# A two-block transformer kernel on one core: the first mixer's head norm and gating spread over three engines, level sums by halves, two modulation rows moved, and both output projections in three rounded passes

## The chip, the core and the metric

The kernel runs on one core of a Trainium2 chip. Its engines work in parallel, each through its own list of instructions in order, and wait for one another on semaphores: TensorE (PE in the profile, with PEld for its weight loads), VectorE (DVE), ScalarE (ACT), GpSimd (POOL) and SyncE (SP), which here only issues transfers. The metric is the device time of one launch, in microseconds.

## What is computed

Two transformer blocks in float32 for 256 tokens of width 1024. The first one has a feed-forward layer, a mixer and a second feed-forward layer, all modulated by nine rows made from a conditioning vector `c`; the second has another mixer and a layer that picks experts. The parts that matter here, cut:

```python
# modulation: nine rows of 1024, 18 tiles of 512 columns in the kernel
mod = (silu(c) @ ada_w + ada_b); (sh1, sc1, g1, sh2, sc2, g2, sh3, sc3, g3) = split(mod, 9)

def head_rmsnorm(h, g, n_heads):            # over 128 columns of each head
    hf = h.reshape(B, S, n_heads, W // n_heads)
    hf = hf * rsqrt(mean(hf * hf, axis=-1, keepdims=True) + EPS)
    return hf.reshape(B, S, W) * g

def token_mix(...):                         # the first mixer
    hm = mlstm_chunkwise(q, k, v, log_i, log_f)          # 4 heads, "scores"
    out_m = head_rmsnorm(hm, mnorm_g, 4) * sigmoid(mo)
    ho = hgrn2_chunkwise(hq_, hk_, hv_, hlf)             # 4 heads, "scan"
    out_h = head_rmsnorm(ho, hnorm_g, 4) * silu(hg)
    return concatenate([out_m, out_h]) @ w_out           # output projection 1

# second block
merged = sigmoid(gate_fox) * (y_fox @ p_fox) + sigmoid(gate_rwkv) * (y_rwkv @ p_rwkv)
x = layer_norm(alpha * x + merged @ w_o, ...)            # output projection 2
```

## The kernel before, in words

**Tiles.** The 256 tokens are two tiles (`TT` = 2) of 128 partitions, the width is eight tiles of 128 (`KT` = 8). All weights of the stages up to the experts form one stream of 1 MB chunks. SyncE loads them in order into a ring of four slots. Chunk g may be loaded when chunk g-3 has begun on TensorE (semaphore `begun`). So what follows a chunk in the stream is fetched only as TensorE goes on.

**Two ways to multiply.** In the plain way float32 operands go to TensorE, and each matmul stands in the trace as two records. In the other, `three_passes` (lines 375 to 377), each operand is a rounded top and a rounded rest, and three matmuls give top by top, top by rest and rest by top. The top of a chunk is made by two ScalarE copies (`top_chunk_act`, line 342), the rest by two VectorE subtractions (`rest_chunk_dve`, line 353), and for the first chunk of some stages by two GpSimd subtractions (`first_rest_pool`, line 951). The feed-forward and input projections are in three passes. The two output projections (`output_pe`, line 590) are plain: eight of the width tiles, two token tiles and two halves of 512 columns make 32 matmuls each.

**The first mixer**, after its input projections:
- *Scores.* `M_SEQ` gives the order in which TensorE works: S (scores of a head, lines 1170 and 1171), T (its transposition, 1176), N (values, 1183 to 1185). VectorE weights the scores, ScalarE copies the transposed ones, and VectorE writes each head's result into `yb` (1424).
- *Scan.* Eight steps i, four heads by two token tiles. TensorE makes the decays of step i+1 (`decays`, 1192), ScalarE takes their exponentials (1306), VectorE multiplies them into queries and keys (`decay`, 1433 and 1435), TensorE multiplies these at eight levels (`attend`, 1208), VectorE masks (`mask`, 1444) and adds the eight levels with one reduction (1451), TensorE multiplies by the values (`read_out`, 1219 and 1221) and VectorE copies out (1458). Steps 1 and 3 also host modulation tiles 14 and 15 (`LOOPED`).
- *Tail.* After the last step TensorE computes modulation tiles 12 and 13 (`BEHIND["scan"]`; one is a group of matmuls with weights from two chunks, lines 667 and 674, and a sum, line 681). Meanwhile VectorE squares all heads (1473), adds (1474), asks ScalarE for the root, and for each token tile multiplies by the inverse root, the gain and the gate (1477 to 1480). TensorE transposes the result, ScalarE copies it to `yT`, and the output projection runs.

**The second mixer** ends similarly. After a long recurrence in four groups VectorE normalises the last group (`group_scale_dve` 1682, 1683, `group_finish_dve` 1689 to 1693), TensorE multiplies it (line 1925, four parts), VectorE merges (2165, 2168), TensorE transposes, and the second output projection starts. GpSimd has nothing to do in either mixer, apart from the first rest of a stage.

## Time and profile before

| what | us |
|---|---|
| median of three runs | 1899.54 (1897.96 to 1906.75) |
| the profiled execution | 1899.65 |
| its span, first to last instruction | 1897.9 |
| TensorE busy | 1785.5 (94%) |
| scores of the first mixer | 368.5 to 380.3 |
| its scan | 380.3 to 430.4 |
| its tail, to the start of the output projection | 430.4 to 445.1 |
| first output projection | 445.1 to 472.8 |
| second output projection | 997.0 to 1024.7 |

The profiled execution is 1.75 us longer than its span. The stages' bounds are read from the instructions in order of time.

### The profile page before, as it was taken

Reading aid. Unit: us, or ns where it says so; the run is one execution under the profiler, and the core shown is the slowest. Engines: PE = TensorE matmul, PEld = TensorE weight load, DVE = VectorE, ACT = ScalarE, POOL = GpSimd, SP = SyncE. Lnnn points to the kernel's source line nnn. Section 1 sums busy time; section 2 is a strip of 40 time slices with the busy share of each in tenths; the row PEclk is TensorE's granted clock in tenths of the full one; section 3 lists DMA queues with packets and bytes.
Section 4 is the critical chain, followed back from the end, with each engine's and each line's share of the span. In section 5 each row is a group of like instructions: output and inputs, shape, how many; then the busy total and the mean of one; then the engine's idle time right before and its main releaser. Section 6 shows DMA issues by size and latency. Waiting matters only on the chain.

```text
span 1897.9 us, 32765 instructions
## 1 busy us (share of the span) xinstructions
PE 1785.5 (94%) x12730; PEld 1552.3 (82%) x12730; DVE 1181.6 (62%) x2035; ACT 764.8 (40%) x1164; POOL 339.9 (18%) x314
## 2 busy tenths in 40 slices
PE   6899989898899989998988999999999999999997
PEld 3899769763799879877855999899999988888885
DVE  3777547594555445874553399948888954444444
ACT  3343344522544445641102454454444443333334
POOL 1000000000000000000000077830000045555553
PEclk9999989999999989999998999999999999999999
DMA  7776555325655534440013445554444466666664
GB/s 305 286 284 246 207 196 178 133 89 210 222 177 177 190 112 139 161 144 21 3 45 133 157 145 169 165 155 146 141 142 141 145 183 194 190 196 190 195 191 155
DMA packets 62368, 315.97 MB, mean 166 GB/s; under 512 B 6928, under 2 KB 7344, under 8 KB 41008
## 3 DMA queue, kind: packets, MB, share of 16 engines
q1 hardware_dynamic: 60912, 305.94, 48.8%
q10 hardware_dynamic: 1280, 8.39, 1.2%
q8 instruction: 84, 1.38, 0.3%
q14 instruction: 28, 0.23, 0.0%
q0 software_dynamic: 64, 0.04, 0.0%
HBM read 313.29 MB, written 1.05 MB: 166 GB/s over the span
## 4 chain that ended last, share of the span: by engine, by line
PE 76%; DVE 9%; DMA 7%; ACT 4%; POOL 2%; issue 2%; SPq 0%; DVEq 0%; POOLq 0%; ACTq 0%
PE bank L375 20%; PE bank L376 20%; PE bank L377 20%; DMA ring<-in_stream 5%; PE bank L590 3%; PE bank L2327 3%; DVE ring_rounded L353 2%; DVE field L845 2%; POOL ring_rounded L2619 1%; DMA ring<-in_experts 1%; ACT arena_rounded L342 1%; PE bank L2301 1%; PE bank L536 1%; PE bank L1925 1%; PE bank L1738 1%
## 5 line engine op out<-in xcount | busy, mean ns | idle before, releaser
L377 PE MATMUL bank<-yb_rounded,ring_rounded 128*128 128x256 f32 x2080 | 595.7, 286 | 0.0
L377 PEld LDWEIGHTS bank<-yb_rounded,ring_rounded 128*128 128x128 f32 x2080 | 406.6, 195 | 0.0
L2425 ACT CAST ring_rounded<-ring 128x1024 fp32r<-128x1024 f32 x250 | 262.5, 1051 | 279.3 <-DMA ring<-in_experts 279.3
L353 DVE TENSOR_TENSOR ring_rounded<-ring,arena_rounded 128x1024 fp32r<-128x1024 f32 x218 | 256.9, 1221 | 163.6 <-ACT arena_rounded L342 163.4
L375 PE MATMUL bank<-yb_rounded,arena_rounded 128*128 128x256 f32 x1104 | 323.3, 293 | 21.5 <-POOL ring_rounded L951 8.2
L376 PE MATMUL bank<-yT_rounded,arena_rounded 128*128 128x256 f32 x1104 | 320.1, 290 | 0.0
L375 PE MATMUL bank<-yb_rounded,ring_rounded 128*128 128x256 f32 x976 | 283.2, 290 | 9.1 <-POOL ring_rounded L2619 6.5
L342 ACT CAST arena_rounded<-ring 128x1024 fp32r<-128x1024 f32 x222 | 221.3, 1047 | 142.0 <-PE bank L375 112.3
L2578 DVE TENSOR_TENSOR ring_rounded<-ring,ring_rounded 128x1024 fp32r<-128x1024 f32 x128 | 157.1, 1227 | 191.7 <-ACT ring_rounded L2425 191.7
L376 PE MATMUL bank<-yT_rounded,ring_rounded 128*128 128x256 f32 x976 | 275.9, 283 | 0.0
L376 PE MATMUL bank<-ring_rounded,arena_rounded 128*128 128x512 f32 x688 | 267.8, 389 | 0.0
L375 PEld LDWEIGHTS bank<-yb_rounded,arena_rounded 128*128 128x128 f32 x1104 | 220.2, 199 | 26.5 <-issue 9.9
L2619 POOL TENSOR_TENSOR ring_rounded<-ring,ring_rounded 128x1024 fp32r<-128x1024 f32 x46 | 125.3, 2738 | 640.6 <-ACT ring_rounded L2425 640.6
L376 PEld LDWEIGHTS bank<-yT_rounded,arena_rounded 128*128 128x128 f32 x1104 | 219.9, 199 | 0.5
L375 PE MATMUL bank<-ring_rounded,arena_rounded 128*128 128x512 f32 x512 | 199.6, 390 | 1.1 <-POOL arena_rounded L2637 1.1
L377 PE MATMUL bank<-ring_rounded,arena_rounded 128*128 128x512 f32 x512 | 199.3, 389 | 0.0
L375 PEld LDWEIGHTS bank<-yb_rounded,ring_rounded 128*128 128x128 f32 x976 | 186.7, 191 | 11.7 <-ACT field L2436 6.5
L376 PEld LDWEIGHTS bank<-yT_rounded,ring_rounded 128*128 128x128 f32 x976 | 187.0, 192 | 0.2
L2634 POOL CAST arena_rounded<-field 128x256 fp32r (+1 forms) x128 | 100.4, 784 | 409.0 <-PE bank L375 409.0
L376 PEld LDWEIGHTS bank<-ring_rounded,arena_rounded 128*128 128x128 f32 x688 | 129.2, 188 | 26.9 <-issue 0.5
L375 PEld LDWEIGHTS bank<-ring_rounded,arena_rounded 128*128 128x128 f32 x512 | 96.1, 188 | 22.6 <-issue 2.8
L377 PEld LDWEIGHTS bank<-ring_rounded,arena_rounded 128*128 128x128 f32 x512 | 96.1, 188 | 20.1
(411 smaller groups left out, 2611.5 us busy)
## 6 DMA issues: line engine op xcount, KB each, us to landing
ring<-in_stream SPq DMA_DIRECT2D x160, 1024.0 KB, 4.9
ring<-in_experts SPq DMA_DIRECT2D x256, 512.0 KB, 3.6
field<-in_gains ACTq DMA_DIRECT2D x1, 2048.0 KB, 7.9
field<-in_gains ACTq DMA_DIRECT2D x1, 1536.0 KB, 6.5
const<-in_const SPq DMA_DIRECT2D x1, 1474.0 KB, 7.9
xh<-in_x ACTq DMA_DIRECT2D x1, 1024.0 KB, 5.6
field<-in_gains ACTq DMA_DIRECT2D x2, 512.0 KB, 6.8
field<-in_norms ACTq DMA_DIRECT2D x1, 1024.0 KB, 9.0
```

The source lines that it names most:

```text
L342: nc.scalar.copy(top, ring[:, g % SLOTS, half * HALF:(half + 1) * HALF]).then_inc(sem("weight_top_ready"), 1)
L353: ins = nc.vector.tensor_tensor(ring_r[:, g % SLOTS, half], ring[:, g % SLOTS, half], top.bitcast(F32), ALU.subtract)
L375: first = pe.matmul(bank, s_top, m_top, start=start, stop=False)
L376: pe.matmul(bank, s_top, m_rest, start=False, stop=False)
L377: return first, pe.matmul(bank, s_rest, m_top, start=False, stop=stop)
L590: ins = pe.matmul(four[2 * t + n][:, :], yT[:, c + k, t * P:(t + 1) * P], w[:, k, :], start=(c + k == 0), stop=(c + k == KT - 1))
L845: nc.vector.scalar_tensor_tensor(row(tile), w[:, k, :], col("c")[:, 4 * c + k:4 * c + k + 1], row(tile), ALU.mult, ALU.add).then_inc(sem(" ...
L2327: ins = pe.matmul(bank[:, q * P:(q + 1) * P], hot[:, g % 2, 0, q, :], hot[:, g % 2, 1, q, :], start=True, stop=True)
L2425: nc.scalar.copy(expert_top[:, n % E_SLOTS, :], expert_w[:, n % E_SLOTS, :]).then_inc(expert_top_ready, 1)
L2578: vec.tensor_tensor(expert_rest[:, slot, :], expert_w[:, slot, :], expert_top[:, slot, :].bitcast(F32), ALU.subtract).then_inc(v_split, 1)
L2619: nc.gpsimd.tensor_tensor(expert_rest[:, slot, :], expert_w[:, slot, :], expert_top[:, slot, :].bitcast(F32), ALU.subtract).then_inc(u_spl ...
L2634: nc.gpsimd.tensor_copy(h_top[:, b, :], src).then_inc(h_top_ready, 1)
```

## The change

Five things are edited.

1. **Head squares on ScalarE, gates on GpSimd.** The squares of each head are summed by ScalarE as the head is done (`score_squares_act`, `loop_squares_act`). GpSimd first multiplies the gates by the gains (two instructions of 1024 elements per partition) and then each finished head by its gate (four instructions of 256, eight of 128). Of the tail are left the root, one reciprocal and one multiplication per token tile.
2. **Level sums by halves.** Two additions (512, then 256 elements) take the place of the reduction of 1024. They leave two partial sums, and `read_out` does one more matmul in each step.
3. **Modulation tiles 12 and 13** move from behind the scan into `M_SEQ`, between the scores. Their chunks move forward in the stream.
4. **Output projections in three rounded passes**, with splits of their four chunks and of the transposed activations.
5. **Early splits.** The first chunk of output projection 1 gets its top at step 5 of the scan and its rest from GpSimd. The first two of projection 2 get theirs behind the last root of the recurrence's norm, also with GpSimd.

The core of the diff:

```diff
     for k in range(4):
-        ins = pe.matmul(four[2 * t + n][:, :], yT[:, c + k, t * P:(t + 1) * P], w[:, k, :],
-                        start=(c + k == 0), stop=(c + k == KT - 1))
+        ins, last = three_passes(pe, four[2 * t + n][:, :], (y_top[:, t, c + k, :], y_rest[:, t, c + k, :]), w[k],
+                                 c + k == 0, c + k == KT - 1)
...
+        def gate_heads_pool(pool):
+            pool.wait_ge(sem("norms_in"), 16)
+            for n, gates in enumerate(("score_gates", "loop_gates")):
+                pool.wait_ge(*marks[gates])
+                at = slice(n * W1, (n + 1) * W1)
+                nc.gpsimd.tensor_tensor(mixg[:, :, at], mixg[:, :, at], norms[:, at].unsqueeze(1).broadcast_to([P, TT, W1]),
+                                        ALU.mult).then_inc(sem("gates_scaled"), 1)
...
+            for i in range(HEADS * TT):
+                if i == 5:
+                    first_rest_pool(pool, "out", "mixed")
+                pool.wait_ge(sem("h_squared"), i + 1)
...
+                nc.gpsimd.tensor_tensor(yb[:, t, at], yb[:, t, at], mixg[:, t, at], ALU.mult).then_inc(sem("h_gated"), 1)
...
         def read_out(i):
-                ins = pe.matmul(bank[:, 0:P], att[:, 0, i % 2, :], val[:, t, :], start=True, stop=not t)
+                pe.matmul(bank[:, 0:P], att[:, i % 2, 0, :], val[:, t, :], start=True, stop=False)
+                ins = pe.matmul(bank[:, 0:P], att[:, i % 2, 1, :], val[:, t, :], start=False, stop=not t)
...
         def mix_act(act):       # in the scan's loop over i
+                if i < 2:
+                    score_squares_act(2 + i)
+                if i >= 3:
+                    loop_squares_act(i - 3)
+                if i == 5:
+                    first_top_act(act, "out", "mixed")
...
         def mask(i):
-                vec.tensor_reduce(att[:, 0, i % 2, :], masked.rearrange("p l s -> p s l"), AX_X, ALU.add
+                v(vec.tensor_tensor(masked[:, 0:4, :], masked[:, 0:4, :], masked[:, 4:8, :], ALU.add))
+                vec.tensor_tensor(att[:, i % 2, 0:2, :], masked[:, 0:2, :], masked[:, 2:4, :], ALU.add
                                   ).then_inc(sem("h_att"), 1)
...
             for t in range(TT):
-                v(vec.tensor_tensor(by_head[:, t], by_head[:, t],
-                                    small[:, 160 + t * 8:168 + t * 8].unsqueeze(2).broadcast_to([P, 8, P]), ALU.mult))
-                v(vec.tensor_tensor(yb[:, t, :], yb[:, t, :], norms[:, 0:D], ALU.mult))
-                vec.tensor_tensor(yb[:, t, :], yb[:, t, :], mixg[:, t, :], ALU.mult).then_inc(sem("y_mixed"), 1)
+                vec.tensor_tensor(by_head[:, t], by_head[:, t], head_inverse[:, t, :].unsqueeze(2).broadcast_to([P, 2 * HEADS, P]),
+                                  ALU.mult).then_inc(sem("y_mixed"), 1)
+            after_first_rest_dve("out", "mixed")
+            turn_split_dve(dve, turned_at["mixed"])
+            for _ in range(3):
+                rest_chunk_dve(dve)
...
         def mix2_act(act):
             group_root_act(act, NCH // GRP - 1)
-            turn_act(act)
+            first_top_act(act, "out2", "merged", 2)
+            top_chunk_act(act, 3)
+            turn_split_act(act)
+            for gap in (0, 1):
+                top_chunk_act(act, gap)
```

**Order, TensorE among the scores.** Before, from the first transposed head (L1176 is T, L1170 and L1171 are S, L1183 to L1185 are N):

```order
L1176 MATMUL bank<-const,field 128x128 x3
L1170 MATMUL bank<-field 128x128
L1171 MATMUL bank<-field 128x256
L1183 MATMUL bank<-field 128x128
L1184 MATMUL bank<-field 128x128
L1185 MATMUL bank<-field 128x128
L1176 MATMUL bank<-const,field 128x128 x3
```

Now, from the same place (L1204 is T, L1198 and L1199 are S, L1211 to L1213 are N, L667 and L674 a modulation tile, L681 its sum):

```order
L1204 MATMUL bank<-const,field 128x128 x3
L667 MATMUL bank<-ring,tiny 32x512 x8
L674 MATMUL bank<-field,tiny 32x512
L1198 MATMUL bank<-field 128x128
L1199 MATMUL bank<-field 128x256
L1211 MATMUL bank<-field 128x128
L1212 MATMUL bank<-field 128x128
L1213 MATMUL bank<-field 128x128
L1204 MATMUL bank<-const,field 128x128 x3
L681 MATMUL bank<-field,const 128x512
```

A modulation tile now stands between the first transposition and the third head's scores, and its sum behind the second transposition. Tile 13 follows in the same way before the third N, and its sum before the last.

**Order, GpSimd, from the start to the experts.** Before:

```order
L2725 MEMSET field 128x7168
L2727 DMA field<-in_ada_b 1x16x448
L951 ISA
L951 TENSOR_TENSOR ring_rounded<-ring,arena_rounded 128x1024 x4
L2619 TENSOR_TENSOR ring_rounded<-ring,ring_rounded 128x1024 x46
```

Now:

```order
L952 ISA
L952 TENSOR_TENSOR ring_rounded<-ring,arena_rounded 128x1024 x2
L1109 TENSOR_TENSOR field<-field 128x2x512 x2
L1115 TENSOR_TENSOR yb<-yb,field 128x2x128 x4
L1122 TENSOR_TENSOR yb<-yb,field 128x128 x5
L952 TENSOR_TENSOR ring_rounded<-ring,arena_rounded 128x1024 x2
L1122 TENSOR_TENSOR yb<-yb,field 128x128 x3
L952 TENSOR_TENSOR ring_rounded<-ring,arena_rounded 128x1024 x6
L2702 TENSOR_TENSOR ring_rounded<-ring,ring_rounded 128x1024 x46
```

Between the input stage's rest (the first two of L952) and the experts there are now fourteen gate instructions and, besides the two for the second feed-forward layer, six subtractions of 1024 elements for the output projections.

**Order, ScalarE at the end of the second mixer.** Before, from the last copy of the recurrence:

```order
L1805 COPY field<-bank 128x4x4x16
L1660 ACTIVATE field<-field 128x4x64
L525 COPY yT<-bank 128x4x128 x4
L2022 DMA field<-in_lns 128x2048
L456 ACTIVATE field,small<-xh 128x512
```

Now:

```order
L1879 COPY field<-bank 128x4x4x16
L1734 ACTIVATE field<-field 128x4x64
L348 CAST arena_rounded<-ring 128x1024 x4
L512 CAST yb_rounded<-bank 128x512 x4
L348 CAST arena_rounded<-ring 128x1024 x4
L2101 DMA field<-in_lns 128x2048
```

Four of the casts stand directly behind the last root (L1660 before, L1734 now); the GpSimd subtractions wait for them.

## Rows read from the trace of the kernel before

**Rows 1.** Stage table, scan: from:to, length, PE, PEld, DVE, ACT, POOL busy, PE clock, DMA.

```profile
382.00:430.00 48.00, 41.30 (x244) 29.18 (x242) 46.14 (x55) 12.19 (x24) 0.00 (x0) 0.96 0.24 88
```

**Rows 2.** Instructions in order of time, PE, end of the scores: start, length, idle before.

```profile
379.51 0.49 PE L1183 MATMUL bank<-field 128*128 128x128 f32 x2 [0.57 <-ACT field L1301]
...
380.28 3.17 PE L1192 MATMUL bank<-const,field 128*128 128x512 f32 x8
```

**Rows 3.** Chain of waits: a modulation tile in the scan, and its sum.

```profile
390.90 1.85 PE bank L667 x16
392.75 0.84 PE bank L674 x2
...
397.97 0.86 PE bank L681 x2
```

**Rows 4.** Groups of the scan: busy, mean ns, idle before and its releaser.

```profile
L1451 DVE TENSOR_REDUCE field<-field 128x128 f32<-128x1024 f32 x8 | 15.4, 1923 | 0.3
...
L1208 PE MATMUL bank<-field 128*128 128x128 f32 x128 | 17.2, 292 | 3.3 <-DVE field L1438 2.1 <-DVE field L1435 0.9 <-DVE field L1444 0.3
```

**Rows 5.** In order of time: ends of the tail on DVE, then the projection.

```profile
430.44 2.29 DVE L1473 TENSOR_TENSOR field<-yb 128x2048 f32<-128x2048 f32 x1
...
442.01 1.22 DVE L1480 TENSOR_TENSOR yb<-yb,field 128x1024 f32<-128x1024 f32 x1
...
445.11 27.73 PE L590 MATMUL bank<-ring,yT 128*128 128x512 f32 x64 [0.72 <-ACT yT L525]
```

**Rows 6.** One pass of 512 columns (chain), and a chunk's two casts on ACT.

```profile
367.32 0.23 PE bank L375
...
1012.77 1.99 ACT L342 CAST arena_rounded<-ring 128x1024 fp32r<-128x1024 f32 x2
```

**Rows 7.** DVE and POOL where both work, in time; one line's min/median/max.

```profile
1136.71 2.38 POOL L2619 TENSOR_TENSOR ring_rounded<-ring,ring_rounded 128x1024 fp32r<-128x1024 f32 x1 [0.32 <-ACT ring_rounded L2425]
...
1136.77 4.46 DVE L2503 TENSOR_TENSOR field<-field,const 128x2048 f32<-128x2048 f32 x1
...
1145.68 2.29 DVE L2508 TENSOR_REDUCE field<-field 128x128 f32<-128x2048 f32 x1
...
1153.20 4.07 POOL L2619 TENSOR_TENSOR ring_rounded<-ring,ring_rounded 128x1024 fp32r<-128x1024 f32 x1 [0.59 <-ACT ring_rounded L2425]
...
1534.28 0.74 POOL L2637 TENSOR_TENSOR arena_rounded<-field,arena_rounded 128x256 fp32r<-128x256 f32 x1 [0.19 <-POOL arena_rounded L2634]
...
L2503 DVE TENSOR_TENSOR field<-field,const x4: 2291/2292/4462, 1136.8 to 1224.1; 128x2048 f32<-128x2048 f32 x4
...
L2501 DVE TENSOR_SCALAR field<-field x4: 502/1568/2329, 1135.7 to 1219.4; 128x128 uint32<-128x128 uint32 x4
```

**Rows 8.** End of the second mixer in order of time, ACT, DVE and PE.

```profile
980.08 0.42 ACT L1660 ACTIVATE field<-field 128x256 f32<-128x256 f32 x1 [7.88 <-DVEq L1676]
...
982.31 0.43 DVE L1683 TENSOR_TENSOR field<-field 128x256 f32<-128x256 f32 x1
982.77 0.98 DVE L1689 TENSOR_SCALAR field<-field,cols 128x64 f32<-128x64 f32 x4
...
984.25 0.42 DVE L1693 TENSOR_TENSOR field<-field 128x256 f32<-128x256 f32 x1
...
994.39 0.69 DVE L2168 TENSOR_TENSOR yb<-yb,field 128x512 f32<-128x512 f32 x1
...
984.73 8.83 PE L1925 MATMUL bank<-ring,field 128*128 128x512 f32 x16 [2.79 <-DVE field L1693]
...
996.96 27.73 PE L590 MATMUL bank<-ring,yT 128*128 128x512 f32 x64 [0.73 <-ACT yT L525]
```

**Rows 9.** Stage table in stretches of 3 us: seventh number is PE's granted clock.

```profile
424.00:427.00 3.00, 2.67 (x14) 2.47 (x12) 2.97 (x4) 0.00 (x0) 0.00 (x0) 0.61 0.00 0
...
487.00:490.00 3.00, 2.82 (x15) 2.83 (x16) 1.32 (x2) 2.38 (x3) 0.12 (x1) 0.63 0.48 115
...
1034.00:1037.00 3.00, 2.03 (x9) 2.04 (x10) 1.19 (x3) 1.44 (x3) 0.00 (x0) 0.50 0.28 41
```

More of the change, by code:

```diff
@@ L275, in top_slot @@
         def top_slot(stage, i):
+            if stage in ("out", "out2"):
+                return top_slots[stage][i % 3]
             special = {"mix": 0, "ffn": FT + FT // 2 - 1}
@@ L1166, in mix_pe @@
             for what, h in M_SEQ:
+                if what == "row":
+                    ada_groups_pe(pe, h)
+                if what == "sum":
+                    ada_sum_pe(pe, h, but=1)
                 if what == "S":
@@ L1298, in mix_act, with square_act, score_squares_act, loop_squares_act @@
             nc.scalar.activation(t_em, t_nm, ACT.Exp).then_inc(sem("m_weights"), 1)
-            for h in range(HEADS):
-                bank = A.get(act)
-                nc.scalar.copy(sT[:, h % 2, :], bank[:, 0:3 * P]).then_inc(A.free, 1)
+            def square_act(t, h, junk):
+                return nc.scalar.activation(act_junk[:, junk % 8 * P:(junk % 8 + 1) * P], by_head[:, t, h, :], ACT.Square,
+                                            accum_out=head_squares[:, t, h:h + 1])
+            def score_squares_act(h):
+                act.wait_ge(sem("m_out"), h + 1)
+                square_act(0, h, 2 * h)
+                square_act(1, h, 2 * h + 1).then_inc(sem("m_squared"), 1)
+            def loop_squares_act(i):
+                act.wait_ge(sem("h_out"), i + 1)
+                square_act(i % TT, HEADS + i // TT, i).then_inc(sem("h_squared"), 1)
+            for what, h in M_SEQ:
+                if what == "row":
+                    ada_groups_act(act, h)
+                if what == "sum":
+                    ada_sum_act(act, h)
+                if what == "T":
+                    bank = A.get(act)
+                    nc.scalar.copy(sT[:, h % 2, :], bank[:, 0:3 * P]).then_inc(A.free, 1)
+                if what == "sum":
+                    score_squares_act(h - 12)
             for i in range(HEADS * TT):
```

110 lines of the change are left out of this document (72 added, 38 removed).

## The prediction, made before the result was known

> **What bounds the kernel now.** I read the chain of waits first, to see which engine ends each stage, then each stage's instructions in order of time. Over the whole launch the chain is mostly TensorE, but the change touches places where others set the pace. In the scores TensorE waits for copies: the last N waits 0.57 us, and the scan's first decays start at 380.28 [rows 2]. In the scan TensorE (41.3 of 48 us) and VectorE (46.1) are both nearly full [rows 1]; until 416.8 TensorE stands still for under 1 us, after that VectorE alone sets the pace. In the tail VectorE is the chain: from its squares at 430.44 to the last gate's end at 443.23, and the projection starts at 445.11 [rows 5]. Then TensorE works 27.73 us without a gap. The second mixer ends in a chain VectorE (to 984.67), TensorE, VectorE, and the second projection starts at 996.96 [rows 8]. GpSimd idles in all of this, so what is moved to it looks free. It shares something with VectorE, though, and this decides the forecast.
>
> **Scores: the two modulation tiles.** One tile is 1.85 + 0.84 us and its sum 0.86 [rows 3]; two make 7.1 us. TensorE's waits in the scores can cover little of that: the longest one, before the first T, lies ahead of the place where tile 12 stands. Behind it there are 1.55 us (one wait of 0.41, two like the 0.57 [rows 2]). Two new waits arise, since N waits until all of ScalarE's banks are copied, and the third N now stands right behind tile 13, the last behind its sum: a copy of about 0.6 and 0.3 of latency each. What is covered is given back: **+7.0** to the scan's start (387.3), +5.5 if both new waits vanish.
>
> **Scan: the level sums.** The reduction takes 1.92 us [rows 4]. An addition of 512 with both inputs in SBUF takes 0.69, one of 256 takes 0.43 [rows 8]: 0.8 less per step, 6.4 in eight. But until step 4 TensorE is as full as VectorE, it gets one more matmul (0.22) per step, and tiles 14 and 15 stay there. I count only the last three steps and a little: **-2.6** (bounds -6.4 and +1).
>
> **Scan: ScalarE.** It gets a square of 128 columns per step, about 0.5 with its read-out, which fits. At step 5 it also casts a whole chunk (1.99 [rows 6]) ahead of the exponentials of step 6, and the square ahead of both waits until VectorE is nearly ready for them. VectorE then stands for about as long as the cast: **+2.2** (bounds 0 and 2.5).
>
> **Scan: the port.** Where VectorE and GpSimd work at once, rows 7 show one waiting for the other's whole instruction. GpSimd starts at 1136.71 and takes 2.38, its usual time. VectorE's addition-like instruction starts 0.06 later and takes 4.46 instead of 2.29: it waits 2.2 and then runs. At 1153.20 VectorE is ahead and GpSimd's instruction takes 4.07. A tensor-scalar instruction goes from 0.50 to 2.33. The reduction at 1145.68 is not held (2.29). So two inputs from SBUF are held, one input for a reduction is not, and a tensor-scalar within SBUF is. In the scan VectorE's decay products (2.2 us a step) have two SBUF inputs, and so have the new additions, where the reduction had one. GpSimd brings per head 0.74 for 256 elements [rows 7], an estimated 0.47 for 128 (worked out between that and 2.38 for 1024), and the rest of the first chunk, 4.7 us in two pieces. The squares that release a gate come just as VectorE begins a decay product, so each gate is caught between two of these. In the first steps the delay partly hides behind TensorE. The rest is asked for behind the fifth gate, at step 7, where nothing hides it: 2.3 us before the second decay product and some 1.5 before the addition. Laid out step by step I get **+5.3**; the ends are 0 (no hold) and 8.5 (all GpSimd work: two heads, five gates, one rest).
>
> Of this the Trainium skill, page "SBUF — State Buffer", section "Who interferes with whom", says that GpSimd and a VectorE instruction with two SBUF inputs, or in a two-port mode, exclude each other for a whole instruction, and that a reduction never contends. By that rule the halves give up what the reduction had; without it the sum would be 13 us lower. The rows agree (4.46 against 2.29).
>
> **Tail.** Before: 430.4 to 445.1, 14.7 us [rows 5]. Now, from the last copy-out: square 0.5, root 0.2, last gate and reciprocal 0.5, two products of 1.22, transposition 0.5, ScalarE's top 0.5 with latency, VectorE's rest 0.65 (new), some latency: 6.5 us. TensorE's modulation work no longer keeps it busy here. Its clock was already down to 0.61 at 424 [rows 9], and now the last attend, read-out and transpositions run at that: +1.2. Together **-7.0** (bounds -8.2 and -6).
>
> **Output projection 1.** 32 products in three passes of 512 columns are 96 x 0.227 = 21.8 us (0.227 is the mean between neighbouring starts, of which one is shown) [rows 6], against 27.73: -6.0. A chunk is used for 5.4 us, and its cast and subtraction (2.0 + 1.2 behind the cast) begin when the chunk ahead begins, so they stay covered; if not, it would be 1 us at most per chunk. But TensorE comes from 9 us of near idleness. After a similar gap, at 487, its clock stood at 0.63 for 3 us and recovered during the next three; that cost some 2.1 us. **-3.9** (bounds -6.0 and 0).
>
> The next stage waits for a chunk from memory, asked for when the projection's chunks begin; it now begins earlier by less than the projection ends earlier: **+0.3** (0 to 0.7).
>
> **Output projection 2.** Again -6.0. The turn gets a subtraction: +0.8. And the port: ScalarE's casts come right behind the root at 980.08, and from 981.6 GpSimd has four subtractions of 2.35 us in a row. On VectorE the chain goes through 1683, the four of 1689, one more product and 1693, all in SBUF, until 984.67 [rows 8]. Each of them finds GpSimd in front, and each lets it in again behind. Four times 2.35 less the 0.7 that a reciprocal (one input, not held) covers is 8.7 us. If the tensor-scalars of 1689 are not held, three waits remain, one of them partly covered: 5.2. I take **+8.0**, as rows 7 show a tensor-scalar held. The clock is a little lower than before: **+0.5** (0 to 2.1). Together +3.3.
>
> **The sum.** 7.0 - 2.6 + 2.2 + 5.3 - 7.0 = +4.9 at the start of projection 1, then -3.9, +0.3 and +3.3: **+4.6 us**. The profiled execution took 1899.65, the median is 1899.54, so they are alike: I predict **1904 us**. What the change saves, it mostly gives back at places where the saved engine was not alone.
>
> **The rivals.**
> - *No hold.* If GpSimd's instructions here slip between VectorE's, the two port terms (5.3 and 8.0) go: 1904.3 - 13.3 = 1891, with well covered rows 1888. For it: its instructions are short, and VectorE has 1.3 to 2 us of bank work in each step. Against: 4.46 and 2.33 in rows 7. 16%.
> - *TensorE hides more.* The tiles among the scores cost 5.5, the halves gain 4, the cast at step 5 is covered: 1904.3 - 1.5 - 1.4 - 2.2 = 1899. Against it: TensorE has no wait behind the first T to hide them in. 12%.
> - *A cold TensorE* (slower). The clock is 0.50 at 1034 [rows 9], and it stayed there from 1028 to 1040 after a similar gap. If both projections start like that, 12 us at half clock cost 6 each instead of 2.1 and 0.5: 1904.3 + 3.9 + 5.5 = 1914. It decides from 5 us more than in my sum, that is if the low clock lasts over 9 us in one or 5 us in both. For it: the tail's cover is taken away. Against: in three passes TensorE is as busy as at 487, where it recovered sooner. 14%.
> - *The passes are no faster* (the change not doing what it says): were weight loads of 0.19 not hidden behind passes of 0.23, both projections would lose their 6 us: 1916. 2%.
>
> **How the numbers follow.** My own case has 56%, with 1897 to 1911 around it from the bounds above. The range of 8 in 10 goes from 1889 to 1912: it takes in more than half of the first rival and leaves out most of the cold one and the slow passes. What a measurement here can tell is about 0.5%, 9.5 us, so faster means under 1890 and slower over 1909. Faster: half of the first rival (8%) and the lower edges of the second and of my own case (5%), 13%. Slower: the last two rivals (16%) and the upper edge of my own case (3%), 19%. Within: 68%.
>
> **What would show it.** In the changed profile: the scan starts about 387; GpSimd's two subtractions near step 7 with decay products or additions of twice their length; VectorE idle before step 6; under 8 us from the last copy-out to projection 1, which takes 22 to 24 us with a clock under 1.0 at first; behind the last root of the second mixer, a tensor-scalar or product of over 2 us, and the merge matmuls starting 5 to 9 us later against the root. The forecast is wrong if VectorE's durations there are unchanged, if the scores absorb the tiles, or if the clock stays at half through a projection.

## The result

The changed kernel takes **1905.84 us** (median of 19 runs, 1898.38 to 1911.09), the kernel before 1900.21 (19 runs, 1891.52 to 1906.75). The ratio is **1.0032, with a 95% interval from 1.0019 to 1.0045**: slower by 0.3%, which is under the 0.5% that the prediction called distinguishable. The forecast was 1904. The profiled executions have spans of 1903.9 and 1897.9 us, so the two traces (6.0 us apart) show a difference like that of the medians (5.6).

A table by stage, read from the instructions in order of time, in us. A stage that is named by its work ends with its last instruction; the other rows are the stretches between:

| stage | before | after | difference | forecast |
|---|---|---|---|---|
| scores: first S to first decays | 11.76 | 20.42 | +8.7 | +7.0 |
| scan: to the end of the last copy-out | 50.13 | 53.66 | +3.5 | +4.9 |
| tail: to the start of projection 1 | 14.70 | 8.12 | -6.6 | -7.0 |
| projection 1 | 27.73 | 23.74 | -4.0 | -3.9 |
| to the start of feed-forward 2 | 14.34 | 14.85 | +0.5 | +0.3 |
| last group root (ScalarE, end of the second mixer) to projection 2 | 16.88 | 26.15 | +9.3 | +8.8 |
| projection 2 | 27.73 | 24.67 | -3.1 | -5.5 |

The rest is unchanged code: from feed-forward 2 to the last group root it took 492.9 us before and 491.0 after, and the stage ahead of the scores ended 0.7 us earlier.

Three places of the trace after carry the reading. All rows are instructions in order of time: start, length, engine, line, operands, count, and in brackets the idle time before with its releaser. First VectorE and GpSimd at the end of the scan. Line 1504 to 1509 are the decay products (line 1509 the small one of a second token tile), 1515 the mask, 1522 and 1523 the two additions that replace the reduction of [rows 4], and GpSimd's line 1122 is a gate, line 952 the rest of a chunk:

```profile
429.92 1.23 DVE L1506 TENSOR_TENSOR field<-field 128x896 f32<-128x896 f32 x1
431.07 2.42 DVE L1509 TENSOR_TENSOR field<-field 128x128 f32<-128x128 f32 x1
433.42 1.27 DVE L1515 TENSOR_TENSOR field<-bank,const 128x512 f32<-128x512 f32 x2
434.73 1.54 DVE L1522 TENSOR_TENSOR field<-field 128x512 f32<-128x512 f32 x1
...
429.02 1.19 POOL L1122 TENSOR_TENSOR yb<-yb,field 128x128 f32<-128x128 f32 x1 [4.37 <-ACT field L1332]
430.17 5.55 POOL L952 TENSOR_TENSOR ring_rounded<-ring,arena_rounded 128x1024 fp32r<-128x1024 f32 x2
...
433.55 3.47 PE L1236 MATMUL bank<-field 128*128 128x128 f32 x16 [4.38 <-DVE field L1509]
```

Line 1509 takes 0.28 us elsewhere and 2.42 here: it waits for GpSimd's first half, which itself had waited for line 1506. The mask, which reads a PSUM bank, is of its usual length. The addition of 1522, two inputs from SBUF, takes 1.54 instead of 0.69. TensorE stands for 4.38 us (2.24 at the same place in e3_vec below, where GpSimd has no subtractions).

The end of the second mixer, to be read against [rows 8]:

```profile
979.66 0.42 ACT L1734 ACTIVATE field<-field 128x256 f32<-128x256 f32 x1 [7.88 <-DVEq L1750]
...
980.11 1.76 DVE L1756 RECIPROCAL field<-field 128x256 f32<-128x256 f32 x1 [0.54 <-ACT field L1734]
981.90 1.82 DVE L1757 TENSOR_TENSOR field<-field 128x256 f32<-128x256 f32 x1
983.76 7.03 DVE L1763 TENSOR_SCALAR field<-field,cols 128x64 f32<-128x64 f32 x4
990.82 0.42 DVE L1766 TENSOR_TENSOR field<-field 128x256 f32<-128x256 f32 x1
991.28 0.42 DVE L1767 TENSOR_TENSOR field<-field 128x256 f32<-128x256 f32 x1
...
981.09 9.42 POOL L952 TENSOR_TENSOR ring_rounded<-ring,arena_rounded 128x1024 fp32r<-128x1024 f32 x4 [492.52 <-ACT arena_rounded L348]
...
991.76 2.93 PE L1999 MATMUL bank<-ring,field 128*128 128x512 f32 x3 [10.23 <-DVE field L1767]
```

Four tensor-scalars of 64 elements took 0.98 us before and 7.03 now. Taken one by one they took 2.21, 2.38, 2.38 and 0.30 us: three stood behind a subtraction each, and the fourth ran as soon as GpSimd's last one was over (990.5). What follows has its old length. From the root to the merge matmuls it is 12.10 us instead of 4.65.

Third, the clock where the tail ends and projection 1 begins (stage table; the seventh number is the granted clock of TensorE):

```profile
441.00:444.00 3.00, 0.59 (x3) 0.29 (x2) 1.46 (x3) 0.76 (x4) 1.16 (x3) 0.50 0.94 336
444.00:447.00 3.00, 2.63 (x13) 2.63 (x14) 1.46 (x3) 0.63 (x2) 0.00 (x0) 0.50 0.37 156
...
450.00:453.00 3.00, 2.96 (x7) 2.38 (x8) 1.00 (x1) 2.07 (x3) 0.00 (x0) 0.50 0.42 74
453.00:456.00 3.00, 3.00 (x13) 2.38 (x13) 3.00 (x4) 1.82 (x2) 0.00 (x0) 0.90 0.67 281
```

0.50 is the lower of TensorE's two levels, 1.00 the upper. It lasts until some 3.4 us into the projection, then the clock is back.

### The profile page after: what moved, and what is told of

Read it like the earlier page. It is cut to its first block, busy times and chain, and to the rows that moved or that the text cites. A ratio compares the mean times of both kernels' runs of the same rounds, so it can differ in the third digit from the quotient of the medians.

```text
span 1903.9 us, 33044 instructions
## 1 busy us (share of the span) xinstructions
PE 1778.9 (93%) x12810; PEld 1569.7 (82%) x12810; DVE 1197.5 (63%) x2054; ACT 785.1 (41%) x1213; POOL 361.3 (19%) x334
## 4 chain that ended last, share of the span: by engine, by line
PE 75%; DVE 9%; DMA 7%; ACT 4%; POOL 3%; issue 2%; SPq 0%; DVEq 0%; POOLq 0%; ACTq 0%
PE bank L381 21%; PE bank L382 20%; PE bank L383 20%; DMA ring<-in_stream 5%; PE bank L2410 3%; DVE ring_rounded L359 3%; POOL ring_rounded L2702 2%; DVE field L845 2%; DMA ring<-in_experts 2%; ACT arena_rounded L348 1%; PE bank L1999 1%; PE bank L542 1%; PE bank L1812 1%; PE bank L667 1%; PE bank L2384 1%
## 5 line engine op out<-in xcount | busy, mean ns | idle before, releaser
L359 DVE TENSOR_TENSOR ring_rounded<-ring,arena_rounded 128x1024 fp32r<-128x1024 f32 x228 | 270.0, 1227 | 174.1 <-ACT arena_rounded L348 174.0
L381 PE MATMUL bank<-yb_rounded,arena_rounded 128*128 128x256 f32 x1104 | 322.5, 292 | 20.4 <-POOL ring_rounded L952 7.1
L348 ACT CAST arena_rounded<-ring 128x1024 fp32r<-128x1024 f32 x238 | 237.0, 1047 | 156.3 <-PE bank L381 127.3
L381 PEld LDWEIGHTS bank<-yb_rounded,ring_rounded 128*128 128x128 f32 x976 | 187.5, 192 | 12.7 <-ACT field L2519 7.2
L952 POOL TENSOR_TENSOR ring_rounded<-ring,arena_rounded 128x1024 fp32r<-128x1024 f32 x10 | 24.3, 2454 | 777.6 <-ACT arena_rounded L348 777.6
L2717 POOL CAST arena_rounded<-field 128x256 fp32r (+1 forms) x128 | 91.7, 716 | 417.4 <-PE bank L381 417.4
L382 PEld LDWEIGHTS bank<-ring_rounded,arena_rounded 128*128 128x128 f32 x688 | 129.2, 188 | 27.0 <-issue 0.5
L381 PEld LDWEIGHTS bank<-ring_rounded,arena_rounded 128*128 128x128 f32 x512 | 96.1, 188 | 21.3 <-issue 1.1
```

What stands on the lines that cost most here:

```text
L348: nc.scalar.copy(top, ring[:, g % SLOTS, half * HALF:(half + 1) * HALF]).then_inc(sem("weight_top_ready"), 1)
L359: ins = nc.vector.tensor_tensor(ring_r[:, g % SLOTS, half], ring[:, g % SLOTS, half], top.bitcast(F32), ALU.subtract)
L381: first = pe.matmul(bank, s_top, m_top, start=start, stop=False)
L382: pe.matmul(bank, s_top, m_rest, start=False, stop=False)
L952: ins = nc.gpsimd.tensor_tensor(ring_r[:, slot, half], ring[:, slot, half], top.bitcast(F32), ALU.subtract)
L2717: nc.gpsimd.tensor_copy(h_top[:, b, :], src).then_inc(h_top_ready, 1)
```

## Experiments

Two theories stood against each other. **The port**: GpSimd's subtractions hold VectorE for whole instructions, in the scan and in the second mixer, and this eats what the passes and the shorter tail give. **The rest**: the added work itself (tiles among the scores, the cast in the scan, more turns) eats it. All times below are medians of several runs where not said otherwise; ratios are to the kernel before on the same chip. The chips differed between experiments and the kernel before had medians of 1898.58 to 1900.21 us on them, so two experiments are best compared by their ratios. A stage's length is read from one profiled execution of each kernel.

**e1_subs and e2_sets: the port on its own, in the kernel before.** GpSimd makes four subtractions of 1024 elements whose results nobody uses, behind the last group root; in e2_sets they are memsets of 2700 elements:

```diff
+            pool.wait_ge(sem("group_root"), NCH // GRP)
+            for n in range(4):
...
+                nc.gpsimd.tensor_tensor(arena2[:, 3 * D:4 * D], arena2[:, 5 * D:6 * D], arena1[:, 4 * D:5 * D],
+                                        ALU.subtract).then_inc(sem("extra"), 1)
```

> The kernel before, plus four GpSimd subtractions of 1024 elements on unused data, released by the last root of the second mixer's norm; nothing else is changed and nobody needs their results before the layer norm. Measured as the time from that root's start on ScalarE to the first of the sixteen merge matmuls behind it on TensorE: 4.65 us before, 12.10 us in the changed kernel. Theory (GpSimd holds VectorE's products and tensor-scalars for whole instructions): 12 to 13 us here too, with the products and the four tensor-scalars together some 7.5 us longer. Rival (the delay in the changed kernel comes from ScalarE's casts or from the chunks' arrival): 4.65 us, all VectorE durations unchanged.

> As the run with four subtractions, but the four GpSimd instructions only write (a memset of 2700 elements, about as long, 2.3 us). The same stretch, root to merge matmul, 4.65 us before. If only GpSimd's reads are shared with VectorE's second input, the products keep their 0.43 us; the tensor-scalars, if they run in a mode that writes two results at once, are held and the stretch is 7 to 12 us. If GpSimd work of any kind holds both, it is as long as with the subtractions, 12 to 13 us, products included. If writes hold nothing, 4.65 us.

One run each: 1910.79 and 1903.25 us, beside 1898.58. The stage shows more than the total. Of e1_subs, then of e2_sets:

```profile
983.76 9.77 POOL L2735 TENSOR_TENSOR field<-field 128x1024 f32<-128x1024 f32 x4 [493.41 <-ACT field L1660]
...
986.42 4.91 DVE L1689 TENSOR_SCALAR field<-field,cols 128x64 f32<-128x64 f32 x4
991.37 2.44 DVE L1692 TENSOR_TENSOR field<-field 128x256 f32<-128x256 f32 x1
```

```profile
981.68 9.63 POOL L2735 MEMSET field<- 128x2700 f32 x4 [493.88 <-ACT field L1660]
...
983.45 0.42 DVE L1683 TENSOR_TENSOR field<-field 128x256 f32<-128x256 f32 x1
983.91 2.72 DVE L1689 TENSOR_SCALAR field<-field,cols 128x64 f32<-128x64 f32 x4
986.66 0.43 DVE L1692 TENSOR_TENSOR field<-field 128x256 f32<-128x256 f32 x1
```

With nothing of the change in it, the kernel before now needs 11.06 us from the root (983.27) to the merge matmuls (994.33), 6.4 more than without. Theory had asked for 12 to 13; GpSimd started 0.04 us behind the reciprocal here and 0.98 behind it in the changed kernel, so the reciprocal covered more of the first subtraction. Memsets of the same total length cost 1.7 us (981.21 to 987.60, 6.39 instead of 4.65, a little under the expected 7): the products with two inputs keep 0.42 and 0.43, and the four tensor-scalars together are held for about the rest of one memset. So GpSimd being busy is not enough: the products are held by an instruction that reads SBUF and not by one that only writes, the tensor-scalars by both. The Trainium skill ("SBUF — State Buffer", section "Who interferes with whom") says that a VectorE instruction with two SBUF inputs excludes only GpSimd instructions that read SBUF, while tensor-scalars may run in a two-port mode, which excludes both kinds. The two traces agree in each of these rows.

**e3_vec: the change without GpSimd's subtractions.** VectorE makes the first chunk's rests of both projections, the rest of the change is kept:

```diff
-                if i == 5:
-                    first_rest_pool(pool, "out", "mixed")
...
-            after_first_rest_dve("out", "mixed")
+            first_rest_dve(dve, "out", "mixed")
...
             merge_dve(1, 0).then_inc(sem("y_merged"), 1)
+            first_rest_dve(dve, "out2", "merged")
...
-            for n in range(2):
-                first_rest_pool(pool, "out2", "merged", n)
```

> The changed kernel with the rests of the first chunks of both output projections made by VectorE: for the first projection behind the two last products, for the second one in VectorE's wait between two merges and behind the turn. GpSimd keeps the gates. Theory (port): root to merge matmul falls from 12.10 to about 4.7 us, the scan (first decays to last copy-out) from 53.7 to about 50.5, the tail grows by 0.8; in all 9 to 11 us less than the changed kernel's 1905.8, so 1895 to 1897. Rival (the delays are ScalarE's casts): the stretches stay, 1905 or more.

Measured 1894.07 us (12 runs), ratio 0.9975 (0.9958 to 0.9991): 11.8 us less than the changed kernel by the medians, 10.8 by the ratios, a little faster than the kernel before, and as expected of the port. The scan takes 50.65 instead of 53.66, root to merge 4.65 instead of 12.10. Its rows there:

```profile
982.60 0.98 DVE L1761 TENSOR_SCALAR field<-field,cols 128x64 f32<-128x64 f32 x4
...
984.55 0.70 PE L1997 MATMUL bank<-ring,field 128*128 128x512 f32 x1 [2.79 <-DVE field L1765]
```

**e13_scanrest: which place it was.** The same, for projection 1 alone.

> The changed kernel with only projection 1's first rest on VectorE; GpSimd keeps its four subtractions at the end of the second mixer. It parts the two places at which GpSimd's subtractions hold VectorE. Theory: the scan falls by what e3_vec's fell, from 53.66 to 50.65 us, the tail stays at 8.2, and the second mixer's end stays at 12.1 us from the last group root to the first merge matmul: 1902.9, ratio to the kernel before 1.0014; the other 8.8 us of e3_vec's gain belong to the second mixer. Rival, that the scan's 3 us come back in its wake (the next stage waits for its chunks anyway) and all of e3_vec's gain was made in the second mixer: 1905 to 1906, ratio 1.003.

Measured 1902.59 us (12 runs), ratio 1.0019 (1.0005 to 1.0032). Scan 50.66, root to merge 12.11. The scan's subtractions cost 3.0 us of its length. By the medians the total fell by 3.2 us, by the ratios by 2.5, and the intervals overlap, so the total alone doesn't exclude the rival. The stages speak against it: from the first score matmul to feed-forward 2 the profile has 117.4 us against 120.8 in the changed kernel, so nothing is given back up to there. The larger part of e3_vec's gain belongs to the second mixer (ratio 1.0019 against 0.9975).

**e4_early: the tiles among the scores.** Tile 12 is moved one place up, into TensorE's wait ahead of the first T:

```diff
-        M_SEQ = [("S", 0), ("S", 1), ("T", 0), ("row", 12), ("S", 2), ("N", 0),
+        M_SEQ = [("S", 0), ("S", 1), ("row", 12), ("T", 0), ("S", 2), ("N", 0),
```

> The changed kernel with modulation tile 12 one place earlier among the scores, ahead of the first transposition, where TensorE stands 2.4 us. If the tiles cost what they add to a full TensorE, the scores (first score matmul to first decays, 20.4 us in the changed kernel, 11.8 before) shrink by 2.4 to 3.5, and the time to about 1903. If they cost by ScalarE's copies and the waits behind them, the scores stay at 20 and so does the time.

Measured 1903.58 us (12 runs), ratio 1.0025 (1.0011 to 1.0039), 2.3 less than the changed kernel by the medians and 1.3 by the ratios, with overlapping intervals: the total doesn't show the gain, the stage does. The scores fall from 20.42 to 16.99 us. Only part of this is the wait (1.8 us against the 18.81 of e12_top); the other part is the clock. In the changed kernel tile 12 ran on the lower level, right behind that wait of 2.41 us (granted clock 0.61 from 372 to 376). In e12_top (below), whose scores are the same code, it did not. After, then e12_top:

```profile
371.72 0.90 PE L1204 MATMUL bank<-const,field 128*128 128x128 f32 x3 [2.41 <-DVE small L1476]
372.55 3.17 PE L667 MATMUL bank<-ring,tiny 128*32 128x512 f32 x16
```

```profile
375.09 0.55 PE L1202 MATMUL bank<-const,field 128*128 128x128 f32 x3 [2.41 <-DVE small L1473]
375.56 1.92 PE L667 MATMUL bank<-ring,tiny 128*32 128x512 f32 x16
```

e12_top and e14_fp32 have scores of 18.81 and 18.82 us with full-speed tiles; e3_vec, e11_red, e13_scanrest and e16_nogates 20.3 to 20.5 with the slow one. In e12_top the clock had fallen earlier (0.57 from 364 to 368) and was at 1.00 from 368 on; in e14_fp32 it was at 1.00 from 360 to 384.

**e12_top: ScalarE's cast at step 5**, moved behind the scan's last exponentials, in e3_vec:

```diff
-                if i == 5:
-                    first_top_act(act, "out", "mixed")
+            first_top_act(act, "out", "mixed")
             nc.scalar.activation(small[:, 500:501], small[:, 500:501], ACT.Sqrt)
```

> e3_vec with ScalarE's cast of projection 1's first top (two of 0.99 us) moved from the scan's step 5 to behind its last step, ahead of the load of the square root's table. It tells what the cast costs in the scan. Theory: it holds the exponentials of one step by 1.98 us, and that step's decays products, so the scan falls by 1.5 to 2.2 us, from 50.65 to about 48.8, with the tail unchanged at 8.3 (ScalarE idles there 0.9 us before each square): 1892.2. Rival, that the cast stands in ScalarE's idle time (it has 2.9 us before the sum at 419.5): scan unchanged, 1894.

The scan takes 48.98 us, 1.7 less, with the tail unchanged at 8.25. The total, 1894.58 us (10 runs, ratio 0.9972, 0.9961 to 0.9983), doesn't show it against e3_vec's 1894.07: 1.7 us is within what these intervals leave open.

**e11_red: the halves**, taken back to the reduction in e3_vec:

```diff
-                v(vec.tensor_tensor(masked[:, 0:4, :], masked[:, 0:4, :], masked[:, 4:8, :], ALU.add))
-                vec.tensor_tensor(att[:, i % 2, 0:2, :], masked[:, 0:2, :], masked[:, 2:4, :], ALU.add
+                vec.tensor_reduce(att[:, i % 2, 0, :], masked.rearrange("p l s -> p s l"), AX_X, ALU.add
```

> e3_vec (no subtraction of GpSimd in the scan) with the level sums back to one reduction of VectorE and one matmul less in each read-out. It tells what the halves are worth where nothing holds VectorE. Theory: the two adds in place of the reduction give the scan 2.6 us, so the scan grows from 50.65 to 53 us and the time from 1894.1 to 1896.7. Rival, that TensorE, which in e3_vec's scan waits only 7.0 us in all and mostly at its ends, sets the pace there: scan 50.7 to 51.2, 1894 to 1894.6.

Measured 1896.56 us (12 runs), ratio 0.9984 (0.9969 to 0.9999), scan 53.11: the halves give 2.5 us. The interval overlaps e3_vec's; the stage length is the evidence.

**e16_nogates: GpSimd's small products**, cut to 4 of 128 columns in e12_top, so that the kernel leaves 124 columns of each head ungated. The twelve instructions are all still there, only short.

> e12_top (rests on VectorE, the cast behind the scan) with GpSimd's twelve gate products cut to 4 columns of each head, so that the other 124 columns of each head go ungated and the output is not the reference's. It tells whether the small gate products of GpSimd (0.46 to 1.19 us in e12_top's scan, nine of them) hold VectorE. Theory: they do, and cost the scan 1.0 to 1.5 us: the scan falls from 48.98 to 47.5 to 48.0 us and VectorE's longest decay product falls back to the usual length. Rival, that they slip in while VectorE waits or reads banks, and the remaining growth is ScalarE's squares: scan 48.8 to 49.1. The time of one run can't tell 1 us; the stage's length does.

One run, 1887.94 us beside 1899.29. The scan takes 48.30 us: less than e12_top's 48.98, but by 0.7 and not by 1.0 to 1.5, which lies between the two expectations. Groups of VectorE in the scan, e12_top and then e16_nogates (busy us, mean ns, idle before):

```profile
L1501 DVE TENSOR_TENSOR field<-field 128x1024 f32<-128x1024 f32 x4 | 5.4, 1354 | 2.5 <-ACT field L1358 2.3 <-DVE yb L1527 0.2
```

```profile
L1501 DVE TENSOR_TENSOR field<-field 128x1024 f32<-128x1024 f32 x4 | 4.9, 1224 | 3.1 <-ACT field L1358 2.9 <-DVE yb L1527 0.2
```

These decay products lose their hold (1354 to 1224 ns, 0.5 us in four), and VectorE then waits 0.6 us longer for ScalarE. What is held ahead of another wait costs nothing.

**e14_fp32: the passes**, taken back in both projections of e3_vec (plain matmuls, copies at the turn, no casts and rests):

```diff
-                    ins, last = three_passes(pe, four[2 * t + n][:, :], (y_top[:, t, c + k, :], y_rest[:, t, c + k, :]), w[k],
-                                             c + k == 0, c + k == KT - 1)
+                    ins = pe.matmul(four[2 * t + n][:, :], yT[:, c + k, t * P:(t + 1) * P], w[:, k, :],
+                                    start=(c + k == 0), stop=(c + k == KT - 1))
```

> e3_vec with both output projections back in fp32 by one matmul for each product, with the copies of before at the turn and no casts and rests of their chunks; all else as in e3_vec. It tells what the three rounded passes are worth with all that they bring. Theory: projection 1 takes 27.7 us instead of 23.1 to 23.7 (+4.1 to its end), the turn until its start 3.2 instead of 5.8 (-2.6), and the scan loses the cast of step 5 (-1.7, as in e12_top): about nothing there. Projection 2 +3.1, its turn -0.5 to -2: +1 to +2.6. Together 1895 to 1897, ratio 0.998. Rival, that the passes are worth the difference of the matmuls alone, 64 x (0.867 - 0.683) us in each projection (rates of the profile before) = 11.8 x 2: 1906 or more.

Measured 1900.45 us (11 runs), ratio 1.0008 (0.9995 to 1.0021), 6.4 more than e3_vec by the medians and 6.3 by the ratios, which lies between the two expectations. The first projection told why:

```profile
443.54 29.59 PE L596 MATMUL bank<-ring,yT 128*128 128x512 f32 x64 [0.68 <-ACT yT L531]
...
994.47 27.73 PE L596 MATMUL bank<-ring,yT 128*128 128x512 f32 x64 [0.73 <-ACT yT L531]
```

Behind the short tail plain matmuls start on the lower clock too and need 29.59 us, not 27.73. So the cold start belongs to the short tail, not to the passes, and the passes are worth 6.1 us of projection 1 (29.59 against 23.51) and 3.1 of projection 2 (27.73 against 24.68). At the first turn they cost 2.0 (443.54 - 439.76 = 3.78 against 5.80), at the second 1.3 (3.56 against 4.83), and 1.4 in the scan (49.23 against 50.65, the cast of step 5). By these stages they are worth 4.5 us in all, by the totals some 6.

**e5_back and e10_split: where the tiles cost least.** Both start from e3_vec. e5_back puts both tiles back behind the scan, e10_split only tile 13, with tile 12 ahead of the first T. Both also take the cast of projection 1's first top out of step 5 of the scan and put it behind the tiles, and order the stream of chunks to match. Of e10_split:

```diff
-        M_SEQ = [("S", 0), ("S", 1), ("T", 0), ("row", 12), ("S", 2), ("N", 0), ("T", 1), ("sum", 12), ("S", 3), ("N", 1),
-                 ("T", 2), ("row", 13), ("N", 2), ("T", 3), ("sum", 13), ("N", 3)]
+        M_SEQ = [("S", 0), ("S", 1), ("row", 12), ("T", 0), ("S", 2), ("N", 0), ("T", 1), ("sum", 12), ("S", 3), ("N", 1),
+                 ("T", 2), ("N", 2), ("T", 3), ("sq", 1), ("N", 3)]
...
+            ada_behind_groups_pe(pe, "scan")
+            ada_sum_pe(pe, 13)
...
-                if i == 5:
-                    first_top_act(act, "out", "mixed")
...
+            ada_behind_groups_act(act, "scan")
+            ada_behind_sums_act(act, "scan")
+            first_top_act(act, "out", "mixed", 2)
```

> The changed kernel with the first chunk's rests of both projections on VectorE (as in e3_vec) and, besides, modulation tiles 12 and 13 and their sums back behind the scan, ahead of the turn; the scores are those of before, and the first top of projection 1 is cast behind the tiles' copies. It tells what the two tiles cost among the scores against what they cost in the shortened tail. Theory: the scores fall from 20.4 us to 12 to 13 (-7.9); behind the scan TensorE stands still for about 3 us between the last read-out and the turn, and the tiles take 5.4 + 1.7 us and two copies of ScalarE, so the tail grows from 8.25 us to 12 to 13 (+4.3), part of it given back because TensorE's clock doesn't fall before the projection (-1): 4 to 5 us less than e3_vec, about 1889.5, a ratio to the kernel before of 0.995. Rival, that the tail takes all of the tiles' 7.1 us and the top's cast behind them: the tail is 16 us, 1894 to 1895, no gain over e3_vec.

> As e5_back, but only tile 13 behind the scan; tile 12 among the scores, ahead of the first T, where TensorE waits for ScalarE and VectorE anyway (as in e4_early). Theory: e4_early's two tiles took 17.0 - 11.8 = 5.2 us of the scores, of which tile 12, in the wait, some 1 to 2; tile 13 in the tail, 2.7 + 0.86 us against a stand of 3 us, costs 1 to 2. Scores 13 to 14 us, tail 9.5 to 10.5: 1888 to 1890, the fastest of all, ratio 0.994. Rival, that the two gaps cover nothing (the first T waits longer than the tile hides, and the last tile delays the top's cast): scores 15.5, tail 12, 1893, as e3_vec.

e5_back took 1896.82 us (12 runs, ratio 0.9981, 0.9967 to 0.9996) and missed both expectations: scores 12.69 as expected, but the tail 20.89. TensorE runs out of chunks between the two tiles:

```profile
440.12 1.93 PE L667 MATMUL bank<-ring,tiny 128*32 128x512 f32 x8 [4.56 <-DMA ring<-in_stream]
```

This wait for memory was in neither sum. e10_split, with one tile there, has no such wait and is, with e15_best below, the **fastest kernel of the study: 1887.36 us** (6 runs, 1886.64 to 1892.53), ratio 0.9945 (0.9930 to 0.9961), as expected. Scores 13.22, scan 49.22 (the cast is out of it), tail 10.57. TensorE's rows behind its scan:

```profile
428.04 1.93 PE L667 MATMUL bank<-ring,tiny 128*32 128x512 f32 x16
429.78 1.02 PE L674 MATMUL bank<-field,tiny 128*32 128x512 f32 x2
431.48 1.12 PE L681 MATMUL bank<-field,const 128*128 128x512 f32 x2 [0.68 <-ACT field L685]
432.44 1.91 PE L502 MATMUL bank<-const,yb 128*128 128x128 f32 x16
439.01 0.80 PE L381 MATMUL bank<-arena_rounded,yb_rounded 128*128 128x512 f32 x1 [4.66 <-DVE yT_rounded L524]
```

The turn (line 502) takes 1.91 us at a granted clock of 1.00, 3.67 at 0.50 in the changed kernel. Ahead of it TensorE worked on the tile here (3.33 of the 4 us from 428 to 432), where it had been nearly idle there (0.63 of the 3 us from 442). The projection itself starts on the lower level in both.

**e15_best: the top's cast earlier**, in e10_split.

> e10_split with the cast of projection 1's first top behind the scan's last exponentials, ahead of the load of the square root's table, instead of behind tile 13's sum. In e10_split this cast stands between the sum's copy and the turn's casts, and the projection starts 6.57 us after the turn, against 5.80 in e3_vec. Theory: the chunk has landed by 413 us, so the cast and VectorE's rest lie ahead of the turn, which then takes 5 to 5.8 us: 1886.2 to 1886.6, 0.8 to 1.5 us less than e10_split, ratio 0.994. Rival, that the cast delays the table's load and with it the last squares and the root (in e12_top ScalarE had 5.1 us to spare there, so this is unlikely), or that the turn is bound by the two engines' casts alone: 1887.4, no difference.

The time from the start of the turn to projection 1 falls from 6.57 to 4.25 us and the tail to 8.25. The total, 1887.80 us (5 runs), ratio 0.9946 (0.9932 to 0.9959), equals e10_split's, so of the two forecasts of the time it is the rival's that came true, although the turn fell by more than theory had. Up to feed-forward 2 the profile still has most of the gain (109.1 us from the first score matmul, 111.2 in e10_split). Whether it is taken back later or is lost in the spread is open: the unchanged code from the next wait for a chunk to the last group root takes 499.8 us in e10_split's profile and 502.6 in e15_best's, and between 497.7 and 503.1 in the profiles of the study.

## Why the prediction held, term by term

The number was right, 1904 against 1905.84, and so was its main claim: the saved time comes back at the two places where VectorE's chain meets GpSimd's subtractions. That the number is so close is in part luck: in the pair of profiles the changed stages cost 8.3 us where the sum had 4.6, and unchanged code that happened to be shorter hid 2.4 of it. Not every term was right.

- **Scores, +7.0: right as a mechanism, mis-sized by the clock.** Both new waits were there, 0.68 and 0.69 us, where a copy of 0.6 and 0.3 of latency had been put down (with the 7.1 of the tiles and the 1.55 covered, these terms add up to 7.35, a little more than the 7.0 stated). At full clock the tiles cost 18.81 - 11.76 = 7.05 us. In the profiled execution tile 12 ran on the lower level, and the term measured 8.7. The scores without the tiles vary as well: 11.76 in the kernel before, 12.7 to 12.8 in e1_subs, e2_sets and e5_back, against which the tiles cost 6.1 at full clock.
- **Scan.** The halves: -2.6 predicted, 2.5 measured (e11_red). The cast: +2.2, 1.7 measured (e12_top). The port: +5.3, measured 3.0 for the subtractions (e3_vec, e13_scanrest) and 0.7 for the gates (e16_nogates): too high by 1.6. The prediction had 2.3 and 1.5 us for the subtractions; the trace has 2.14 on line 1509 (2.42 less 0.28) and 0.85 on line 1522 (1.54 less 0.69), the first as foreseen, the second smaller, since more than half of GpSimd's second subtraction ran beside the masks. That left 1.5 for the gates, twice what they measured; some of them are held ahead of a wait for ScalarE. If these effects simply add, 3.5 - (-2.5 + 1.7 + 3.7) leaves 0.6 us that the predicted sum had not. ScalarE's squares, which stand ahead of exponentials, are one candidate; the gates themselves are another, since e16_nogates only shortens them. No run took either out.
- **Tail, -7.0:** -6.6, with the turn on the lower clock, as put down (3.67 us). The last attend, which the prediction counted here, ran on the lower clock too (3.47 us, 2.05 in e3_vec) but lies in the scan.
- **Projection 1, -3.9:** -4.0. Here the step was right by its working: 21.8 us and some 2 for the clock. e16_nogates, whose projection 1 starts on a granted clock of 1.00, took 22.07 for it, so the lower clock cost 1.7 here.
- **Projection 2, +3.3: the term that was mis-sized most.** The projection starts 9.3 us later against the root, where 8.8 had been put down (port 8.0, turn 0.8). The 9.3 are 7.45 of hold, 0.6 of merge matmuls that run slower behind it (9.22 us instead of 8.66) and 1.3 at the turn (4.83 instead of 3.57). The forecast took VectorE's instructions as caught one by one. The trace has them so, 1.82 instead of 0.43, then 7.03 instead of 0.98, but the last tensor-scalar and the last two products slip through, since GpSimd was finished. What failed is the projection's own length: it gained 3.1 us, not 6.0 less 0.5. It starts on a lower clock (0.76 from 1005 to 1008, then 0.67), for which 0.5 had been put down, and there is a wait that the sum hadn't:

```profile
1008.00:1011.00 3.00, 3.00 (x11) 2.39 (x10) 0.00 (x0) 0.00 (x0) 0.00 (x0) 0.67 0.73 306
...
1019.31 0.47 PE L381 MATMUL bank<-arena_rounded,yb_rounded 128*128 128x512 f32 x1 [0.74 <-DVE ring_rounded L359]
```

The third chunk's rest comes 0.74 us late; e3_vec has the same wait of 0.74. Of the 24.67 measured, 21.8 and 0.74 leave 2.1, which is put down to the clock as a remainder. So the second projection cost 6.2 us in all, where 3.3 had been forecast.
- **What made up for it:** the table's differences add up to +8.3. Unchanged code was 1.9 us shorter between feed-forward 2 and the last root, 0.7 ahead of the scores, and 0.2 longer at the end. In other profiles the same instructions differ by over 5 us (and the code ahead of the scores ends anywhere from 366.0 to 373.6), so this is most likely spread and not an effect of the change. By its stages in this pair of profiles the change is worth 8.3 us to the worse; the medians say 5.6, with an interval of 3.6 to 8.6. The sum of 4.6 was low by 2.9 for the second projection and 1.7 for the scores, and high by 1.4 for the scan.

Of the rivals, *no hold* falls by 2.42 us for a 0.28 us instruction and by e1_subs. *TensorE hides more* falls: the scores cost 6.1 to 8.7 by the pairs above, not 5.5, the halves gave 2.5 and not 4, and the cast was not covered (1.7). *A cold TensorE* was half right, since both projections start on a low clock, but it lasts some 3.4 us in each and not over 5. *The passes are no faster* falls by e14_fp32.

The part whose gain didn't show is thus the passes. They save 6.1 us of projection 1 and 3.1 of projection 2, pay 4.7 of it at the turns and in the scan, and bring GpSimd's hold of 3.0 and 7.45, which is more than the rest. With VectorE making the same subtractions in half of the time (2.35 us for two instead of 4.67, beside TensorE's turn and merge), the gain stays.

## What to carry to other kernels

An idle GpSimd is not free for the work of a chain that runs on VectorE: count each of its instructions that reads SBUF as a possible hold of VectorE, look for what VectorE does at that time and whether it waits for something else anyway, and try the same work on VectorE first. Before moving TensorE work into or out of a gap, look at what the gap covers on both sides: the two tiles cost 6 to 9 us among the scores, tile 12 alone 0.5 to 1.5 in a wait (13.22 against the 11.76 to 12.8 of scores without tiles), and in the tail they had also kept TensorE at work, and its clock up, until the projection. Where a stage's length changes by less than some 3 us, read the stage and not the total, and look at the granted clock before reading it.

## What the runs showed of the hardware

- Back-to-back instructions of the two engines took turns. Of four tensor-scalars of 0.3 us, three took 2.21 to 2.38 us beside GpSimd's row of 2.35 us instructions (7.03 for the four), so a chain of short VectorE instructions is a bad place for a hold: the loss goes by GpSimd's length, not VectorE's.
- In e2_sets the write-only GpSimd instructions held the tensor-scalars once (2.72 us for four, 0.98 without) and no product with two inputs.
- Gate products of 4 columns still stood up to 0.95 us on GpSimd in e16_nogates, 0.20 when alone: so GpSimd seems to wait for VectorE's instructions as VectorE waits for its; the 5.55 us of two subtractions at 430.17 (4.67 elsewhere) show the same.
- TensorE's lower clock came behind the same wait of 2.41 us in some profiles and not in others, so the same code shows scores of 18.8 or 20.4 us. The runs don't settle what decides it.
